# Two transformer blocks on one Trainium2 core: packed scores and moved steps in the second block, a part of the modulation on VectorE, later third scores, and the context loaded behind the first weights

## The reference, cut to what matters

```python
def first_block(x, c, ctx, c_ctx, w_ada, b_ada, ...):
    mod_lat = silu(c) @ w_ada + b_ada          # 1024 x 6144; six parts of 1024
    mod_ctx = silu(c_ctx) @ w_ada + b_ada
    sa, sca, ga, sf, scf, gf = split(mod_lat, 6)
    # h = modulate(rmsnorm(x), sa, sca), the same of ctx with csa, csca; then projections
    # dq dk dv (diff), cq ckv kr (latent), q = rmsnorm(cq) @ w_uq, kv = rmsnorm(ckv) @ w_ukv
    # rotary positions on dq, dk, q_rope, kr; attention over ctx and x (512 keys)
    x = x + ga * merge_heads(diff_attend(...), mla_attend(...), w_out)
    hf = modulate(rmsnorm(x), sf, scf)
    x = x + gf * moe(hf, router_w, router_b, w1, b1, w2, b2)     # top 4 of 32 experts
    return rmsnorm(x, final_norm_w)

def second_block(x, ...):
    proj = rmsnorm(x) @ w_in
    y_pool = pool_mixer(u_pool)                 # running means of 2, 4, 8, 16 tokens
    y_dil = dilated_attention(qkv_dil, rel_bias)   # 3 groups x 4 heads, scores + bias table
    y_sb = stick_breaking_attention(qkv_sb)     # 4 heads
    y_s5 = s5_mixer(u_s5)                       # complex linear recurrence over 256 tokens
    merged = sum(sigmoid(xn @ w_gate[i]) * (y_i @ w_branch_i))
    x = x + merged @ w_out
    x = x + (silu(g) * u) @ w_down              # g, u = rmsnorm(x) @ w_up
    return rmsnorm(x)
```

## Time and profile before

| what | us |
|---|---|
| three runs | 1894.57, 1897.06, 1897.45 |
| median | 1897.06 |
| the profiled execution's own time | 1893.97 |
| its span, first to last instruction | 1892.2 |
| first block up to the last value of attention | 0 to 245 |
| x1, router | 245 to 282 |
| routing and experts | 282 to 1232 |
| second block's projections, mixers, gates | 1232 to 1619 |
| x2 and feed-forward net | 1619 to 1892 |

### The profile page before, as it was taken

One profiled execution on the slowest core, in us unless ns is written; L12 is line 12 of the kernel. 1 busy time (PEld: TensorE's weight loads), 2 busy tenths in 40 slices (PEclk: granted clock), 3 DMA queues, 4 the chain that ended last, 5 costly groups with the idle time before them and its releaser, 6 DMA issues.

```text
span 1892.2 us, 20767 instructions
## 1 busy us (share of the span) xinstructions
PE 1712.7 (91%) x8428; PEld 1037.7 (55%) x8428; DVE 450.7 (24%) x1017; ACT 279.7 (15%) x572; POOL 121.3 (6%) x265
## 2 busy tenths in 40 slices
PE   6999999699967989598979799899998999999997
PEld 3634584144322434143424244387776788888886
DVE  5225312022101112022102120255555312121101
ACT  4014312011000101011001010023223300100000
POOL 5760000000000000000000000000020000000000
PEclk9999999899988999799999999999998999999999
DMA  9436479999999999999999999963442335524250
GB/s 379 158 112 253 134 329 386 384 414 414 419 421 416 411 419 419 419 414 414 419 420 417 414 417 419 395 238 112 143 149 103 112 111 200 190 100 178 101 188 23
DMA packets 134068, 547.03 MB, mean 289 GB/s; under 512 B 9180, under 2 KB 21096, under 8 KB 98125
## 3 DMA queue, kind: packets, MB, share of 16 engines
q1 hardware_dynamic: 129248, 529.83, 70.6%
q0 software_dynamic: 4128, 14.42, 2.0%
q10 hardware_dynamic: 588, 1.38, 0.2%
HBM read 540.33 MB, written 7.62 MB: 290 GB/s over the span
## 4 chain that ended last, share of the span: by engine, by line
PE 47%; SPq 19%; DMA 14%; DVE 3%; issue 1%; ACT 1%; POOL 0%; DVEq 0%
SPq L1666 18%; DMA arena<-in_w 10%; PE PS L2225 8%; PE PS L1292 7%; PE PS L2066 4%; PE PS L1317 4%; PE PS L2251 4%; DMA ring<-in_w 4%; PE PS L2087 3%; PE PS L2079 2%; PE PS L1268 2%; PE PS L2215 2%; PE PS L2095 1%; PE PS L1328 1%; PE PS L1302 1%
## 5 line engine op out<-in xcount | busy, mean ns | idle before, releaser
L1292 PE MATMUL PS<-ring,arena 128*64 128x512 f32 (+2 forms) x960 | 292.7, 663 | 61.0 <-DMA arena<-in_w 39.3
L1292 PE MATMUL PS<-arena 128*32 128x512 f32 (+2 forms) x968 | 266.9, 666 | 31.7 <-DMA ring<-in_w 21.1
L1292 PEld LDWEIGHTS PS<-ring,arena 128*64 128x64 f32 (+2 forms) x960 | 84.9, 139 | 205.9 <-issue 205.5
L1317 PE MATMUL PS<-ring,arena 128*64 128x512 f32 (+2 forms) x528 | 151.7, 613 | 14.8 <-DMA arena<-in_w 9.5
L1292 PEld LDWEIGHTS PS<-arena 128*32 128x32 f32 (+2 forms) x968 | 79.2, 140 | 137.8 <-issue 137.6
L2225 PE MATMUL PS<-arena,ring 128*128 128x256 f32 x704 | 152.6, 379 | 0.0
L2225 PEld LDWEIGHTS PS<-arena,ring 128*128 128x128 f32 x704 | 133.5, 190 | 18.0
L1559 DVE TENSOR_SCALAR arena<-PS 128x512 f32<-128x512 f32 x28 | 19.4, 692 | 507.1 <-PE PS L1302 507.1
L1317 PE MATMUL PS<-arena 128*32 128x512 f32 (+2 forms) x424 | 111.6, 631 | 20.6 <-DMA ring<-in_w 13.0
L1317 PEld LDWEIGHTS PS<-ring,arena 128*64 128x64 f32 (+2 forms) x528 | 47.2, 133 | 89.1 <-issue 88.1
L2066 PE MATMUL PS<-arena,ring 128*128 128x256 f32 x384 | 84.9, 380 | 0.0
(11 more groups left out here) (462 smaller groups left out, 2100.0 us busy)
## 6 DMA issues: line engine op xcount, KB each, us to landing
ring<-in_w SPq DMA_DIRECT2D x186, 1024.0 KB, 23.1
arena<-in_w SPq DMA_DIRECT2D x174, 1024.0 KB, 22.9
ring<-in_w_ada SPq DMA_DIRECT2D x24, 1024.0 KB, 7.5
cst<-in_w SPq DMA_DIRECT2D x24, 1024.0 KB, 23.8
ring<-in_w_in SPq DMA_DIRECT2D x22, 1024.0 KB, 9.4
ring<-in_w_up SPq DMA_DIRECT2D x20, 1024.0 KB, 8.2
ring<-in_w_gate SPq DMA_DIRECT2D x16, 1024.0 KB, 7.2
ring<-in_w_down SPq DMA_DIRECT2D x11, 1024.0 KB, 8.3
```

The lines of the kernel that those rows point to most:

```text
L1292: m = pe.matmul(bank(("up", i, b))[rows[n], :], xs[:, k, rows[n]], tiles[n][:, b * 512:(b + 1) * 512], start=k == 0, stop=False, skip_grou ...
L1317: m = pe.matmul(bank(("down", i, c))[rows[n], :], actT[:, k, rows[n]], tiles[n][:, a:a + 512], start=k == 0, stop=k == 7, skip_group_check ...
```

## The change

1. **First loads.** SP issues x, the eight loads of `w_ada`'s first part and the first two of `w_in`, and only then the context, which stood second. `rms ctx` and `h 1` move from before the modulation to behind `dq 1`; the squares of the context go to `hT` and no longer share two buffers with those of x. The tables of constants are reordered: the ones needed first come in a load of 128x640 (1152 columns before), and those of the routing in a load that ScalarE issues at the rotation of `dk 1`.
2. **Second part of the modulation.** The 32 matmuls of `mrow 1 k` are gone. VectorE sums the eight row blocks, each scaled by a column of silu(c) (`add k`: one TENSOR_SCALAR and seven SCALAR_TENSOR_TENSOR of 128x2048), beside `dk 0` to `dk 3`, `cq 0`, `ckv` and `kr`. Row block 0 goes to slot 0 and is summed in place; the others go to slots 1, 1, 1, 1, 2, 1, 2, and SP issues each only after the `add` that empties its slot (`row_added`). Four matmuls of ones against the sum follow behind `dv 1`, and `mcol 1` behind `dv 2`.
3. **Slots.** `w_uq` and `w_ukv` are loaded behind `kr` into slots 4 and 5, part 2 of `w_ada` into slots 3, 2, 1, 0, 6, 7, 4, 5, `w_out` into slots 0 to 3.
4. **Third scores.** `score` of the third unit and `soft` of the second stand behind `qn 0` and `qr 0`, not ahead of them.
5. **Second block.** The three score matmuls of a dilated unit write one bank for t = 0 (128x384) and two for t = 1 (128x512 and 128x256), so VectorE's three additions become one and two. The recurrence's bodies go to n = 2, 5, 8, 11, 17, 21, 28. `bias_of` 0 and 1 go to the head of the recurrence's first step; the pooling products take two PSUM banks of rotation "b" and no longer four of "f". `x2` waits for each part of `mg` by itself.

The diff, cut to its core:

```diff
-        PRE = [("silu",)] + ... + [("rms", "x"), ("rms", "ctx")]
-        PRE += [("mrow", 0, k) for k in range(8)] + [("mcol", 0), ("aw",), ("h", 0), ("h", 1)]
+        PRE = [("silu",)] + ... + [("rms", "x")]
+        PRE += [("mrow", 0, k) for k in range(8)] + [("mcol", 0), ("aw",), ("h", 0), ("ctxsquare",)]
+        BESIDE = {("dk", j): [("add", j)] for j in range(4)}
+        BESIDE.update({("cq", 0): [("add", 4)], ("ckv",): [("add", 5)], ("kr", 0): [("add", 6), ("add", 7)], ("dv", 1): [("mrow", 1, 7)], ("dv", 2): [("mcol", 1)]})
+        FETCH = {("dq", 3): [(0, 0), (1, 1)], ("add", 1): [(2, 1)], ("add", 2): [(3, 1)], ("add", 3): [(4, 1), (5, 2)], ("add", 4): [(6, 1)], ("add", 5): [(7, 2)]}
...
         for j in range(4):
             dense(("dq", j), True)
+            if j == 1:
+                PRE += [("rms", "ctx"), ("h", 1)]
...
-        PRE += [("score",) + UNITS[0], ("score",) + UNITS[1], ("soft",) + UNITS[0], ("score",) + UNITS[2], ("soft",) + UNITS[1]]
+        PRE += [("score",) + UNITS[0], ("score",) + UNITS[1], ("soft",) + UNITS[0]]
         for h in range(4):
             dense(("qn", h))
             dense(("qr", h), True)
+            if h == 0:
+                PRE += [("score",) + UNITS[2], ("soft",) + UNITS[1]]
...
-        side = [one for m in (1, 2) for one in [("mrow", m, k) for k in range(8)] + [("mcol", m)]]
+        side = [("mrow", 2, k) for k in range(8)] + [("mcol", 2)]
...
+                elif kind == "add":
+                    w.wait_ge(slot_in[one.slot], 16 * one.fill)
+                    if k:
+                        w.wait_ge(row_added, T["added", k] - 1)
+                        dve.scalar_tensor_tensor(out=sum_of, in0=slot_view(one.slot), scalar=c2p[:, k, 0:1], in1=sum_of, op0=ALU.mult, op1=ALU.add).then_inc(row_added, 1)
...
-            yield [("s5init",)]
+            yield [("s5init",), ("bias_of", 0), ("bias_of", 1)]
...
-            if n in (1, 5, 9, 13, 17, 21, 25):
+            if n in (2, 5, 8, 11, 17, 21, 28):
...
+        PARTS = [(0, 3)], [(0, 2), (2, 3)]
...
                 if i == 0:
-                    for g in range(3):
-                        plan.group(s + (g,), from_rot("a"))
+                    for a, _ in PARTS[t]:
+                        plan.group(s + (a,), from_rot("a"))
...
-                    w.wait_ge(mg_ready, plan.ups["mg"])
                     for k in range(8):
+                        w.wait_ge(mg_ready, T["mg", (3, k)])
...
             sp.dma_start(xv, I["xT"].rearrange("(k p) t -> p k t", p=128)).then_inc(x_in, 16)
+            load_all(sp, w, plan.loads[:10], pe_done, slot_in)
             sp.dma_start(ctxT, I["ctxT"].rearrange("(k p) t -> p k t", p=128)).then_inc(ctx_in, 16)
-            load_all(sp, w, plan.loads[:MAIN_LOADS], pe_done, slot_in)
+            load_all(sp, w, plan.loads[10:MAIN_LOADS], pe_done, slot_in)
```

151 lines of the change are left out of this document (95 added, 56 removed).

## The result

The changed kernel takes 1871.28 us (median of four runs, 1869.79 to 1871.83), the kernel before 1897.26 in the same comparison. The ratio is 0.9868, with a 95% interval of 0.9853 to 0.9884: some 25 us faster. The forecast was 1869, its range 1861 to 1883. The profiled execution took 1869.79 us with a span of 1867.9, against 1892.2 before: 24.3 us less.

A forecast was written before the change was run, and what follows sets the result against it. DMA was taken to bound from 245 us to the experts' end, TensorE before and from 1232 on. First block -9.1 and second -18.4 gave -27.5, from a median of 1897.06 to a forecast of 1869, range 1861 to 1883.

The forecast's parts named there:

- the first block: Everything up to attention's end: context, modulation, additions and third scores together, forecast at -9.1 us.
- The signs: Profile marks to confirm the forecast: expert loads at about 236, dk 0 1 to 2 us later, additions 2.4, score rows 1.1.
- the five brackets: Second block: five TensorE waits of 1.57, 4.24, 2.88, 2.96 and 1.39 us, together 13.0, expected to vanish.
- What bounds: DMA bounds from 245 us to the experts' end; a microsecond gained before 245 should reach the end in full.
- Rival 4: Expert stream held by something other than attention's end, so only the second block's gain counts: 1878.7; chance 0.03.
- Context behind the first weights: Start of the first block: earlier loads -2.2 us, rms ctx in TensorE's own work +3.5, h 1 about 0.
- Modulation on VectorE: First block: matmuls out of attention -8.4 us, new matmuls and mcol +1.5, additions beside the projections +1.
- rival 3: Additions' chain with slow landings, four loads paid in series; at landings of 15 to 16, slower at 1902; chance 0.03.
- Third scores: Attention's start: idle time and slow matmuls of 6.3 us, 1.8 left in place, so -4.5; bounds 0 and -6.5.
- Second block: Waits -13.0 us, slow rows behind them -6.4, new costs +1: sum -18.4, bounds -20.5 and -8.
- Rival 1: Second block: recurrence bodies hit other softmaxes, the waits move and half of the 18.4 comes back: 1879; chance 0.20.
- Rival 2: First block: additions take 4.8 us beside GpSimd, TensorE waits 9 to 11, the block's gain is gone: 1879; chance 0.15.

The follow-up runs named there:

- e4: Changed kernel, but GpSimd starts the widest step of its first table only after VectorE's eight multiplications of x; 1866.76 us, ratio 0.9842.
- e9: Changed kernel with the context loaded second again, its norm ahead of the modulation, and GpSimd's widest step behind the multiplications of x; 1866.74 us, ratio 0.9854.
- e1: Changed kernel with its first part undone: context the second load, its norm ahead of the modulation, h 1 behind h 0; 1865.86 us, ratio 0.9843.
- e8: Changed kernel with one more 128x2048 VectorE operation ahead of each addition but the first; 1873.14 us, ratio 0.9879.
- e6: Changed kernel with dilated scores unpacked again (one bank and one addition per score), recurrence bodies in their new places; 1878.23 us, ratio 0.9895.
- e10: Changed kernel with recurrence bodies in their old places and scores unpacked; 1882.11 us, ratio 0.9933.
- e2: Changed kernel with the modulation's second part again as TensorE matmuls between attention's units, no additions on VectorE; 1873.65 us, ratio 0.9887.
- e11: Changed kernel with the sums for the sub-norm's root one attention unit later; 1865.89 us, ratio 0.9843.
- e12: Changed kernel with context loaded second again, GpSimd's widest step behind the multiplications of x, and the sub-norm's root one unit later; 1859.93 us, ratio 0.9814.

## Why the prediction came out right

The time lay 2 us above the forecast. The sum was -27.5, the profiles give -24.3. Two sides missed in opposite directions: the first block gave 5.8 for 9.1, the second 20.7 for 18.4. That the total is so near is in part luck, since the first block's 5.8 could have been 11.8, mostly by the clock at one wait.

**The signs.** The profile has no wait at `rms cq`, additions of 2.3 to 2.8 us, none of the five brackets, and a clock of 1.0 where it was 0.56. Three came otherwise: `dk 0` 3.9 us later and not 1 to 2, the first expert loads at 239.6 and not 236, the score row at 1.69 and not 1.1.

**What bounds.** Right. Attention's end releases the experts' loads, and -5.8 us there became -5.4 at the experts' end. Rival 4 is out for the change itself; in e4 and e9 up to 4 us of a larger gain got lost in that stage, for a reason that no run shows.

**Context behind the first weights: wrong by 2.6.** Forecast +1.3 at `dk 0` (-2.2 and +3.5), measured +3.9. The modulation's end came 2.5 sooner, `rms ctx` cost 3.6: both terms right. Two steps were missing. I let `h 0` shift with its start, though the very row that I used for `h 1` (6.72 beside GpSimd, 3.24 without) says that its length hangs on a neighbour that does not shift: 1.6 us. And I left out that TensorE, now waiting for three loads, would be at half clock sooner: that leaves about 1 us. The part was worth less than nothing (e1).

**Modulation on VectorE.** Additions +1 forecast, 0 measured: they took 2.34 to 2.81 us, and add 4's copy of `cq` was done at 101.3, ahead of TensorE's 103.7. Landings of 5.0 were right, and so is that the chain's links count in full (e8). Its start was wrong: I had `add 1` done at 68 and the chain at 90, and they were done at 78.4 and 100.9, since the first two additions stand behind rotations and not behind their loads. So there was a slack of 2 us and not of 10, three loads in series and not the four of rival 3, and with landings of 7.5 it would have been late by some 5 us and not just late (an estimate from the rows above). The new matmuls cost 2.3, not 1.5: they wait 0.78 us for a bank that ScalarE frees. Attention gave -6.7 and not -8.4. The rows were worth more than that (9.9 at equal clock); what I left out was the slow stretch behind a wait of 0.8 us that I had not weighed, because it stood in both kernels. In the five profiles with this first block attention, from its first turn to its last value, gave 6.7 to 11.6 us.

**Third scores: right.** -5.3 measured, -4.5 forecast; the 1.8 that I kept back for new waits was too careful, the whole loss was 6.3, and little of it remained.

**Second block: right in mechanism, mis-sized at the allowance.** -20.7 for -18.4. Idle time and clock sum to 19.4, and the +1 for new waits was not needed; the last 1.3 I can't place. The causes were partly assigned wrong: I gave the wait of 2.9 to the body as much as to the bank, and e6 shows that the bank decides. The bias table's wait had two remedies at once. Rival 1 (waits move) did not happen, but the kernel is one edit away from it: with the scores unpacked the new places have two waits of 2.8 us (e6), though they are still 2.9 us better than the old ones (e10).

**Rival 2 (additions at twice their time).** Out, though GpSimd computed beside them: see below. **Rival 3** out, landings were 5.0.

**Not foreseen:** +1.7 at the norm of the second block, where sixteen matmuls took 5.08 us. All kernels with the additions on VectorE have it (24.8 us from the experts' end to the first projection, 23.1 before), with the bias table early or late. e2 does not: 23.1 us again, and the same sixteen matmuls took 3.70. The changed kernel, then e2:

```profile
1241.48 5.08 PE L2091 MATMUL PS<-arena,ring 128*128 128x256 f32 x16
```

```profile
1244.54 3.70 PE L2090 MATMUL PS<-arena,ring 128*128 128x256 f32 x16
```

So it comes with the second part of the change or with the slots that moved along with it; by what way stays open. One difference ahead of it goes with it, without being shown as the cause: TensorE's last wait for an expert's weights is 1.35 to 1.44 us in the twelve kernels with the loss, and 0.99 (before) and 1.19 (e2) in the two without.

## What to carry to other kernels

Before you move an engine's step forward, look which of its rows are long because of a neighbour, and whether the neighbour moves too; if not, the step may only grow by what it gained. Price a wait of TensorE by the rows behind it as well, and remove even a short one that stands in a busy stage: 0.8 us cost 1 to 6 here (e10, e11). Undo the edits of a bundle one by one and in pairs: of five, one cost time, and two were worth more together than apart. And take more than one profile of the same work before you read a few microseconds out of a place: five with the same first block differed by 6 us at its end.

## What the hardware showed

**Here VectorE and GpSimd took turns by whole instructions.** Short operations of VectorE with two inputs in SBUF beside GpSimd's 1.2 us ones took 1.04 us each for 0.41. But a long one keeps GpSimd out: while `add 2` ran, GpSimd's operation on 16 columns took 2.19 us, and its like 0.22; `add 3` and `add 4` met one of 2.45 (its like 0.40) and one of 2.97 (1.04).

```profile
83.33 2.34 DVE L952 SCALAR_TENSOR_TENSOR ring<-ring,arena 128x2048 f32<-128x2048 f32 x1
```

```profile
83.21 0.27 POOL L709 TENSOR_TENSOR arena<-arena 128x16 f32<-128x16 f32 x1
83.56 2.19 POOL L711 TENSOR_TENSOR arena<-arena 128x16 f32<-128x16 f32 x1
```

So the additions hardly suffered (2.34, and 2.81 at most; only the first, a TENSOR_SCALAR, took 2.28 where it takes 1.28 in e12) and GpSimd's tables ended 11 us later, at 138.5 for 127.5, which nothing waited for. The Trainium skill's page "SBUF — State Buffer", section "Who interferes with whom", says that a VectorE instruction with two inputs in SBUF contends with a GpSimd instruction that reads SBUF, and that the shared port pair is an exclusive lock. That whoever issues first holds it for the whole instruction it says of VectorE's two-port modes. The trace agrees with the lock, for these instructions with two inputs: 2.19 us for GpSimd's beside 2.34 for the addition. My second rival read the contention as a slower rate for both.

**The same idle time costs different amounts.** The wait of 0.81 us at the sub-norm's root was followed by clocks of 1.00, 0.87, 0.74 or 0.61 over 13 us, in kernels most of which differ in attention only in when they come there. What decides it, no run shows. And at 1238 to 1247 the clock was 0.81 in a stretch in which TensorE was busy without a gap:

```profile
1238.00:1247.00 9.00, 9.00 (x52) 8.20 (x53) 1.41 (x8) 1.49 (x2) 0.81 (x2) 0.81 0.86 329
```

Thirty-two matmuls of two columns lie in it, as they did in the kernel before and in e2, where the clock stayed at 1.00 (1242 to 1251, and 1240 to 1250).
